# A transformer block pair on one Trainium2 core: other ring buffers and another order for the FFN's and the modulation's weights, and block products for a 1024x1024 projection

## The reference, cut to what matters

```python
# first block: gated FFN with a causal three-tap convolution, F = 2816
up, gate = h @ w_up            # 1024 x 5632, 22 feature tiles of 128, twice
g = silu(conv3(gate_half)) * other_half
x = x + g @ w_down
# second block: modulation by silu(c) and silu(c_ctx)
mod_lat = silu(c) @ w_mod + b_mod        # 1024 x 6144, all six parts
mod_ctx = silu(c_ctx) @ w_mod + b_mod    # only the first third is used
# second block: convolution branch
y = silu(layer_norm(depthwise_conv31(glu(u))))   # 512 x 1024
y_c = y @ w_pw                                   # 1024 x 1024
out = (sigmoid(g_a) * y_a + sigmoid(g_c) * y_c) @ w_out
```

## Time and profile before

| | us |
|---|---|
| median of 3 runs | 2852.98 (2847.22 to 2857.23) |
| the profiled execution | 2857.41, of which the span from first to last instruction 2856.1 |
| up projection, from unit 1 to the first down product | 432.90 to 697.43 |
| last gates and layer norm to the start of the w_pw product | 1094.6 to 1128.11 |
| w_pw product, norms of the latents | 1128.11 to 1187.22 |
| attention, first PEER tiles | 1187 to 1508 |
| PEER | 1508 to 2856 |

### The profile page before, as it was taken

The page is one execution under the profiler, slowest core; times in us unless marked ns, Lnnn a source line. Parts: engine busy times, 40 slices in busy tenths (PEclk is TensorE's granted clock), DMA queues, the critical chain, the costliest instruction groups (busy, mean ns, idle before and its releaser), DMA issues.

```text
span 2856.1 us, 24271 instructions
## 1 busy us (share of the span) xinstructions
PE 2551.8 (89%) x8286; PEld 1395.8 (49%) x8286; DVE 1713.8 (60%) x3704; ACT 648.4 (23%) x1588; POOL 679.1 (24%) x574
## 2 busy tenths in 40 slices
PE   8999989999999999999998989799877777777776
PEld 5655458887444443466665544365322323232222
DVE  1132449988116993366545676766675767667555
ACT  2223220001011002266412221322121221222112
POOL 0000032332000000000002344444443444444342
PEclk9999999999999999999999999999999999999999
DMA  4101023344212211000249999999999999999997
GB/s 160 59 30 47 13 111 148 148 177 177 103 54 97 89 72 62 15 1 30 88 154 370 420 420 419 405 420 420 420 420 420 420 420 420 420 420 420 420 420 295
DMA packets 87305, 687.01 MB, mean 241 GB/s; under 512 B 9976, under 2 KB 10616, under 8 KB 12816
## 3 DMA queue, kind: packets, MB, share of 16 engines
q0 software_dynamic: 73728, 536.90, 45.5%
q1 hardware_dynamic: 12016, 143.99, 13.1%
q10 hardware_dynamic: 1440, 4.57, 0.4%
HBM read 683.32 MB, written 2.10 MB: 240 GB/s over the span
## 4 chain that ended last, share of the span: by engine, by line
PE 46%; DMA 27%; DVE 5%; ACT 2%; issue 1%; POOL 0%; ACTq 0%; DVEq 0%; POOLq 0%
PE psum L400 21%; DMA weights<-in_experts,expert 16%; PE psum L1113 11%; DMA slot<-in_experts,expert 10%; PE psum L914 3%; PE psum L1007 2%; PE psum L865 2%; PE psum L985 2%; PE psum L936 2%; PE psum L975 2%; PE psum L922 1%; DVE weights L2265 1%; DVE slot L2265 1%; DMA xn<-in_experts,expert 1%; ACT spare_row L1582 1%
## 5 line engine op out<-in xcount | busy, mean ns | idle before, releaser
L1113 PE MATMUL psum<-weights,spare_row 128*128 128x512 f32 x832 | 386.5, 607 | 106.5 <-ACT spare_row L1582 104.3
L1113 PE MATMUL psum<-slot,spare_row 128*128 128x512 f32 x844 | 401.6, 612 | 49.8 <-ACT spare_row L1582 49.7
L2339 POOL DMA_INDIRECT slot<-in_experts,expert x211 | 223.8, 1061 | 577.1 <-DVE expert L2212 304.6
L2265 DVE CUSTOM_DVE_ANT_0 slot<-slot,hT 128x1024 f32<-128x1024 f32 x211 | 257.4, 1223 | 164.3 <-DMA slot<-in_experts,expert 163.0
L2265 DVE CUSTOM_DVE_ANT_0 weights<-weights,hT 128x1024 f32<-128x1024 f32 x208 | 253.5, 1223 | 147.6 <-DMA weights<-in_experts,expert 146.6
L1113 PEld LDWEIGHTS psum<-weights,spare_row 128*128 128x128 f32 x832 | 152.6, 191 | 327.8 <-ACT spare_row L1582 171.5
L2339 POOL DMA_INDIRECT weights<-in_experts,expert x208 | 223.0, 1072 | 298.3 <-PE psum L1113 290.0
L1113 PEld LDWEIGHTS psum<-slot,spare_row 128*128 128x128 f32 x844 | 162.8, 196 | 261.2 <-issue 184.1
L1577 ACT ACTIVATE coef<-hidden 128x2 f32<-128x2 f32 (+1 forms) x257 | 52.2, 203 | 977.6 <-DVE hidden L2265 977.6
L1113 PE MATMUL psum<-xn,spare_row 128*128 128x512 f32 x372 | 188.2, 630 | 86.4 <-ACT spare_row L1582 86.4
L400 PE MATMUL psum<-xnT,weights 128*128 128x264 f32 (+1 forms) x1040 | 246.4, 392 | 6.7 <-DVE gT L1828 2.8
(11 more groups left out here) (361 smaller groups left out, 3279.1 us busy)
## 6 DMA issues: line engine op xcount, KB each, us to landing
weights<-in_w_mod SPq DMA_DIRECT2D x12, 2048.0 KB, 8.3
weights<-in_w_up SPq DMA_DIRECT2D x11, 2048.0 KB, 7.7
weights<-in_w_in SPq DMA_DIRECT2D x8, 2048.0 KB, 8.3
weights<-in_w_pq SPq DMA_DIRECT2D x8, 2048.0 KB, 11.5
weights<-in_w_out SPq DMA_DIRECT2D x6, 2048.0 KB, 9.2
weights<-in_w_in_t SPq DMA_DIRECT2D x4, 2048.0 KB, 7.7
weights<-in_w_down SPq DMA_DIRECT2D x4, 2048.0 KB, 8.4
weights<-in_w_o_mla SPq DMA_DIRECT2D x4, 2048.0 KB, 9.9
```

The costliest lines, as they stand in the source:

```text
L1113: last = pe.matmul(acc.pair[:, half, :], k.diags[pick % 8], k.slots[slot][:, D + half * 512:D + (half + 1) * 512], start=h0 == 0 and j == ...
L2265: ins = dve.tensor_tensor_reduce(slot[:, 0:D], slot[:, 0:D], k.h2[:, i, :], 1.0, 0.0, ALU.mult, ALU.add, hid[:, j:j + 1])
L2339: pool.indirect_dma_start(k.slots[slot], None, k.A["experts"], bass.IndirectOffsetOnAxis(ap=k.expert[b % 2][:, j:j + 1], axis=0))\
```

## The change

Four edits.

1. Ring: the up units take buffers 2 and 0 in turn, and the modulation's units buffer 1 alone. SyncE's order becomes up 0, up 1, mod 0, up 2, mod 1, ...: each up unit one place earlier. The modulation's units are taken in `MOD_ORDER`, so that two-row units (16 instructions) and one-row units (8) alternate.
2. Product order in an up unit: 1, 5, 6, 7, 2, 3, 4 in place of 1, 6, 5, 7, 2, 3, 4, product 5 waiting for s1 alone; GpSimd's sums for unit 1 wait until VectorE has made t1 to t4.
3. `ln_sq`, the PE product that VectorE's sum of squares must precede, goes behind the first tile of `gates(3)`.
4. The w_pw product in block form: per pair of output tiles `q` seven products of 4 matmuls with 256 columns; GpSimd makes the sums of w_pw's blocks (of the first unit once `ln_sq_sum` is complete, of the second once `gates(3)` is done, since they lie over `hT`), VectorE those of the tokens' blocks after the last Silu. ScalarE copies product 1 out, VectorE adds the others. The three latent norms all move into `q` = 2. The attention's `values2` on ScalarE waits for `pw_gated` in place of the last w_pw tile.

```diff
+MOD_ORDER = (0, 4, 1, 5, 2, 6, 3, 7, 8, 9, 10, 11)
+    def mod_rows_of(self, turn):
+        return MOD_ORDER[turn], sum(2 if m < 4 else 1 for m in MOD_ORDER[:turn])
 def ffn_up():            # tensor
+        k.ring.order, k.ring.at = [2, 0, 1] + (NF // 2 - 3) // 2 * [2, 1, 0, 1] + [2, 1, 1], 0
+        k.up_units, k.mod_units = [k.ring.turn()], []
         for u_ in range(NF // 2):
-            unit, w = weights(KC, 512)
-            k.ring.turn()
+            if u_ + 1 < NF // 2:
+                k.up_units.append(k.ring.turn())
+            k.mod_units.append(k.ring.turn())
+        k.ring.order, k.ring.at = [0, 1, 2], 0
...
+                pe.wait_ge(s.up_sum, 4 * u_ + 1)
+                if u_ == 0:
+                    pe.wait_ge(s.up_xsum, 1)
+                product((u_, h, 5), left(sums[0], h), t1)
                 pe.wait_ge(s.up_sum, 4 * u_ + 2)
...
                 product((u_, h, 6), left(sums[1], h), t2)
-                product((u_, h, 5), left(sums[0], h), t1)
 def latents_and_norm():  # tensor
-        u = take("ln_sq")
-        pe.wait_ge(s.ln_sq_sum, KC - 1)
-        pe.matmul(u.pair[:, 0, :], k.ones[:], k.ln_sum, start=True, stop=True).then_inc(u.fill())
-        gates(3)
+        def squares():
+            ...
+        gates(3, squares)    # called behind the first of its four tiles
 def conv_out():          # tensor
+        def product(q, x, left, right, reads=1):
+            u = take(("pw", q, x), reads)
+            chain(u.pair[:, 0, 0:SEQ // 2], [(left[:, c, q % 2, :], right[:, c, :]) for c in range(KC // 2)]).then_inc(u.fill())
+        for q in range(4):
+            product(q, 1, blocks[0], low_left)     # q == 0: then product 2
+            pe.wait_ge(s.pw_sum, q // 2 * 4 + 2)
+            product(q, 5, s1, t1)
+            product(q, 6, s2, t2)
+            if q == 2: feature_norm("n_cq", SEQ, 0, 2)
+            pe.wait_ge(s.pw_sum, q // 2 * 4 + 4)
+            product(q, 7, blocks[2], t3, reads=2)
+            if q: product(q, 2, blocks[1], high_left)
+            if q == 2: feature_norm("n_ckv", SEQ, 2, 1)
+            product(q, 3, s4, high_right)
+            u = product(q, 4, blocks[3], t4)
+            if q == 2: feature_norm("n_ckv_c", CTX, 3, 1)
+            if q == 1: swap()
 def ffn_up():            # vector
-            some(mods, 3 if 0 < u_ < 5 else 2)
+            some(mods, 3 if u_ and MOD_ORDER[u_ - 1] < 4 else 2)
...
-            some(mods, 4 if u_ < 4 else 2)      # twice
+            some(mods, 4 if MOD_ORDER[u_] < 4 else 2)
 def conv_out():          # vector
+        dve.wait_ge(s.ln_silu, KC)
+        dve.tensor_tensor(t1[:], low_right, low_left, ALU.subtract).then_inc(s.pw_xsum)
+        ...                                  # t2, t3 (in place), t4: 128 x 1024 each
+        def blocks(q):
+            plus(k.pw_both[:], k.pw_first[q % 2][:], u[6])
+            plus(one[1], k.pw_both[:], u[5])
+            yield
+            plus(two[1], one[1], u[7]); plus(k.pw_both[:], k.pw_both[:], u[7])
+            plus(one[0], k.pw_first[q % 2][:], u[2])
+            yield
+            plus(one[1], one[1], u[3]);  gated(2 * q, u[2], u[3])
+            plus(two[0], k.pw_both[:], u[4]);  gated(2 * q + 1, u[4])
 def gpsimd_program(k):
         elif u_ == 1:
             pool.wait_ge(*of["xnT2", NT - 1].full[1])
+            pool.wait_ge(s.up_xsum, 4)
         else:
-            pool.wait_ge(*k.ring_done[unit - 4])
+            pool.wait_ge(*k.ring_done[k.up_units[u_ - 2]])
+    for u_ in range(2):
+        pool.wait_ge(s.ln_sq_sum, KC - 1)
+        pool.wait_ge(*k.arrived(k.pw_units[u_]))
+        if u_:
+            pool.wait_ge(*of["gate", 2 * KC - 1].full[-1])
+        ...                                  # s1, s2, low0 - low1, s4, as in ffn_up
 def sync_program(k):
+    weights("w_up", 0)
     for unit in range(NF // 2):
-        weights("w_up", unit)
-        weights("w_mod", unit)
+        if unit + 1 < NF // 2:
+            weights("w_up", unit + 1)
+        weights("w_mod", MOD_ORDER[unit])
```

More of the change, by code:

```diff
@@ L812, in conv_in, with gates @@
             gates(u_)
-    def gates(u_):
+    def gates(u_, behind_first=k.nothing):
         unit, w = weights(KC, 512)
@@ L854, in swap @@
             pe.matmul(u.pair[R, 0, :], k.swap2[R, R], k.kr[R, 0:SEQ], start=True, stop=True).then_inc(u.fill())
-        between = {3: swap, 4: lambda: feature_norm("n_cq", SEQ, 0, 2), 5: lambda: feature_norm("n_ckv", SEQ, 2, 1),
-                   6: lambda: feature_norm("n_ckv_c", CTX, 3, 1)}
-        for n in range(KC):
-            if n % 4 == 0:
-                unit, w = weights(KC, 512)
-            u = take(("pw", n))
-            for c in range(KC):
-                if n == 0:
-                    pe.wait_ge(s.ln_silu, c + 1)
-                last = pe.matmul(u.pair[:, 0, :], w[:, c, n % 4 * P:(n % 4 + 1) * P], k.padded[:, c, 0:SEQ], start=c == 0, stop=c == KC - 1)
-            last.then_inc(u.fill())
+        low_left, low_right, high_left, high_right = k.pw_windows()
@@ L867, in conv_out @@
             k.ring_done[unit] = u.full[-1]
-            if n in between:
-                between[n]()
+            if q == 1:
+                swap()
     def attention():
@@ L1389, in conv_out, with first @@
     def conv_out():
+        def first(q):
+            if q > 1:
+                act.wait_ge(*of["pw", q - 2, 2].free)
+            copy_out(("pw", q, 1), k.pw_first[q % 2][:], of["pw", q, 1].pair[:, 0, 0:SEQ // 2])
+        for q in range(3):
+            first(q)
         act.wait_ge(s.kr, 1)
@@ L1442, in attention @@
         queries(0)
[L1443 removed]
+        act.wait_ge(s.pw_gated, KC)
         values2()
@@ L1773, in mixer, with mod_sums @@
                 add_out(1, half, i)
-    def mod_sums(m):
-        unit = k.mod_unit(m)
+    def mod_sums(turn):
+        m, first = k.mod_rows_of(turn)
+        unit = k.mod_units[turn]
         w = k.weight(unit)[:].rearrange("p (k n) -> p k n", k=KC)
@@ L2001, in conv_out @@
     def conv_out():
-        for n in range(KC):
-            u = of["pw", n]
-            dve.wait_ge(*u.full[-1])
-            dve.tensor_tensor(k.merged[:, n, :], u.pair[:, 0, :], k.sig_c[:, n, :], ALU.mult).then_inc(u.out)
-            if n != 3:
+        low_left, low_right, high_left, high_right = k.pw_windows()
+        t1, t2, t4 = k.pw_xsums
+        dve.wait_ge(s.ln_silu, KC)
+        dve.tensor_tensor(t1[:], low_right, low_left, ALU.subtract).then_inc(s.pw_xsum)
+        dve.wait_ge(s.pw_xsum, 1)
@@ new lines, in conv_out, with plus, gated @@
+        dve.tensor_tensor(t2[:], high_right, t1[:], ALU.subtract).then_inc(s.pw_xsum)
+        dve.tensor_tensor(low_right, high_right, low_right, ALU.subtract).then_inc(s.pw_xsum)
+        dve.wait_ge(s.pw_xsum, 2)
+        dve.tensor_tensor(t4[:], high_left, t2[:], ALU.subtract).then_inc(s.pw_xsum)
+        def plus(dst, left, u):
+            dve.wait_ge(*u.full[-1])
+            dve.tensor_tensor(dst, left, u.pair[:, 0, 0:SEQ // 2], ALU.add).then_inc(u.out)
+        def gated(n, *made):
+            for u in made:
+                dve.wait_ge(*u.free)
+            dve.tensor_tensor(k.merged[:, n, :], k.merged[:, n, :], k.sig_c[:, n, :], ALU.mult).then_inc(s.pw_gated)
@@ new lines, in blocks @@
+        def blocks(q):
+            u = {x: of["pw", q, x] for x in range(1, 8)}
+            one, two = ([k.merged[:, n, a:a + SEQ // 2] for a in (0, SEQ // 2)] for n in (2 * q, 2 * q + 1))
+            dve.wait_ge(*u[1].free)
+            plus(k.pw_both[:], k.pw_first[q % 2][:], u[6])
+            dve.wait_ge(*u[6].free)
+            plus(one[1], k.pw_both[:], u[5])
+            yield
+            dve.wait_ge(*u[5].free)
+            plus(two[1], one[1], u[7])
+            plus(k.pw_both[:], k.pw_both[:], u[7])
+            plus(one[0], k.pw_first[q % 2][:], u[2])
+            yield
+            plus(one[1], one[1], u[3])
+            gated(2 * q, u[2], u[3])
+            dve.wait_ge(*u[7].free)
+            plus(two[0], k.pw_both[:], u[4])
+            gated(2 * q + 1, u[4])
+            yield
@@ new lines, in conv_out @@
+        for q in range(4):
+            steps = blocks(q)
+            next(steps)
+            if q == 2:
+                feature_norm("n_cq", [k.cq[:, 0, :], k.cq[:, 1, :]], SEQ, [col(k, "q_g", 0), col(k, "q_g", 1)], k.feature_root[0])
+            next(steps)
+            if q == 2:
+                feature_norm("n_ckv", [k.ckv[:, 0:SEQ]], SEQ, [col(k, "kv_g")], k.feature_root[1])
+            next(steps)
+            if q == 2:
+                feature_norm("n_ckv_c", [k.ckv[:, SEQ:NKV]], CTX, [col(k, "kv_g")], k.feature_root[2])
+            if q != 1:
```

78 lines of the change are left out of this document (62 added, 16 removed).

## The result

The changed kernel takes 2834.99 us (median of 4 runs, 2831.57 to 2836.62) against 2854.51 (4 runs of the kernel before, 2847.22 to 2857.23): ratio 0.9935, 95% interval 0.9923 to 0.9948, or 19.5 us less. The forecast was 2838, 15 us less. The profiled execution took 2831.57, with a span of 2830.3 against 2856.1, 25.8 us less.

A forecast was written before the change was run, and what follows sets the result against it. PE sets the time before 2000 us, with VectorE nearly as full in the up projection; DMA gathers bound it after. Terms -3.5 - 5.1 - 6.6 = -15.2 us from 2857.41 give 2842.2, or 2838 against the median 2852.98; range 2826 to 2850.

The forecast's parts named there:

- The layer norm's sum: Before w_pw: a gate tile ahead of the squares' product fills PE's 3.40 us gap; -5.1 us, bounds -5.2 and -3.
- The forecast's worst case: Layer norm: GpSimd's sums block the reciprocal and first scaling, token sums end by 1124; cover said to hold by 4 us.
- The w_pw product: Block form: 224 matmuls of 0.217 us take 48.6 us in place of 55.1; -6.6 us, bounds -6.9 and -3.
- The rival that w_pw isn't bound by PE: w_pw is bound by what surrounds it, so its 6.6 us don't come: 2845 us, chance 0.12.
- Unit 0: Up projection: token sums run alone, PE resumes 4.3 us earlier and regains full rate; -6.1 us, bounds -3.5 and -6.3.
- The rival in which the gap stays: Up projection, unit 0: the gap stays because t1 isn't faster alone: 2844 us, chance 0.05.
- Units 1 to 10: Up projection: waits on GpSimd go, waits for VectorE come; stalls 11.4 us in place of 8.8, +2.6; bounds -8.8 and +19.
- the walk: Unit-by-unit timing of VectorE beside GpSimd in the up projection: 3.5 us stall in unit 1, 1.9 in 4, 2.7 in 5.
- A rule against the change: Shared SBUF ports: by the skill's lock rule each GpSimd instruction could wait out a whole VectorE one; rows show about half.
- the slow case: Up projection: GpSimd waits 0.75 us per instruction, VectorE needs 31 us a unit against PE's 25.7: 2863 us, chance 0.04.
- The rival of no stalls: Up projection: VectorE keeps up and no unit stalls; 26.6 us gained in all, 2826 us, chance 0.20.
- The rival of 3.5 us in each unit: Up projection: VectorE sets the pace, 3.5 us stall in each of units 1 to 8, +19; 2854 us, chance 0.11.

The follow-up runs named there:

- e2: The kernel before with only the norm and w_pw edits (3 and 4), up stage as before: 2839.32 us, ratio 0.9958.
- e5: The changed kernel with the first FFN convolution tap moved from VectorE to ScalarE and the second half's shared addition ahead of the convolution: 2828.77 us, ratio 0.9928.
- e12: The changed kernel with the squares' product ahead of the gates again: 2841.95 us, ratio 0.9964.
- e1: The kernel before with only the up projection's edits (1 and 2), norm and w_pw as before: 2850.09 us, ratio 0.9993.
- e6: The changed kernel run again without further change, on the same chip as its variants: 2831.52 us, ratio 0.9937.
- e11: The changed kernel with the old product order 1, 6, 5 in the up units: 2832.46 us, ratio 0.9932.

## Why the prediction was right, point by point

**The layer norm's sum**: right in mechanism and size (-5.1; 36.36 or 36.37 us in every trace with the edit in place of 41.2 to 41.5). The price named, squares later and Silu later, is there, and the cover holds by more than forecast: the token sums end 8 us before PE asks for t1. The forecast's worst case, by its own times (sums done at 1124, t1 wanted at 1126.5), left 2.5 and not the 4 it names.

**The w_pw product**: right (-6.6; 52.52 or 52.53 us in every trace with the edit). PE never waits in it. The forecast feared q = 2 most and put VectorE's end of it at 1170.5 with w_pw's start at 1123, 47.5 us behind it; measured is 1159.6 with the start at 1112.31, 47.3. The rival that w_pw isn't bound by PE fell with this.

**Unit 0**: right in mechanism, too small in size, -7.7 against -6.1 and outside its bounds by 1.4. The forecast's own two terms (411.81 - 407.5, and 5.63 - 3.5) add up to 6.4, so -6.1 is 0.3 too small by its own terms, and the bound of -6.3 is too small as well. t1 alone is 1.23 us, inside the 1.1 to 1.5 estimated, and the instructions behind the gap regained their rate as said. The 1.6 us missed lie ahead of both: in the kernel before PE's first 16 instructions of the stage took 5.38 us at 398.66, in the one after 3.71. They took 3.71 in e2 too, with the up stage as before, and 5.39 in e5 and e12, which have the changed one, so this is no effect of the change. The same sum, made from e2, is 11.48 to 7.32 for the restart plus 6.28 to 3.72 for the instructions behind, -6.7. That is still 0.4 us past the bound. The rival in which the gap stays fell in all eleven traces with both halves of the edit.

**Units 1 to 10**: the forecast total was near and the walk behind it was wrong. Waits for GpSimd went, as said; those for VectorE came, 6.9 us and 1.5 more for the slower instructions behind the longest. Against the 255.7 without stalls the stage is 9.5 us longer, where 11.4 was forecast. But the walk put the large ones in units 1, 4 and 5, and they came in 1 and 3, with 0.35 and 1.13 us in 7 and 8. In unit 1 all three of its first sums had started before GpSimd did, at +8.35 us (433.32) and not +7.8, so `right5` was in time and only `right7` late, 1.54 us in place of 3.5. In unit 3 VectorE came in at +7.8 (485.75) where the walk had +5.5, behind the start of GpSimd's first instruction and not before it, and the `right5` forecast for +13.0 came at +19.2 (497.20). The step that failed is the state carried from unit to unit. The other traces of this up stage say that this is not chance alone: in all four VectorE is done with the gates at +6.8 to +10.2 of unit 3, and PE stalls there for 3.0 to 4.6 us where the walk had none; in units 4 and 5 it is done at +4.1 to +6.0 where the walk had +6.8 and +6.6, and PE stalls for 0.24 us at most where the walk had 1.9 and 2.7. That the total came out near (9.5 for 11.4) is therefore luck in part: the 4.6 us forecast for units 4 and 5 didn't come, and 3.9 us with 1.5 more behind them came in unit 3, where none were forecast. Beyond that a walk can't be sure of single units: in unit 3 only 0.6 us decide between VectorE's sum and GpSimd's (485.75 and 485.15), the point on which, as the forecast says itself, all hangs, and single waits for modulation weights are longer (1.96 us at 454.86). The range for the total (from all stalls gone to 19 more) was wide against what four traces span, 6.5 us.

**A rule against the change.** The traces show VectorE held (50 us of held time in the up stage). GpSimd's instructions start 2.3 to 2.4 us apart alone (1087.28, 1094.31 and the two between) and up to 3.0 beside VectorE, mostly 2.6 to 2.8, so 0.3 to 0.6 us more and not the 0.75 of a whole VectorE instruction each time; the slow case that rested on it, 2863, fell. The Trainium skill (SBUF — State Buffer, "Who interferes with whom") has the pair of ports locked for the whole instruction by whichever engine came first, and the other fully blocked. This is no evidence against that rule: a held sum ends 0.3 to 0.55 us behind GpSimd's instruction, and that is about what GpSimd's next one waits. What failed is the 0.75 that the slow case took for each wait.

**The rival of no stalls** (2826) isn't this change, but it is a measured kernel: 2827.07 and 2826.87 us, once with VectorE relieved and once with GpSimd. **The rival of 3.5 us in each unit** (+19 in the stage) comes nearest with the plain order of modulation units, +10.4 in units 1 to 10 against the kernel before.

**The sum.** 15.2 us less forecast, 18.8 in the changed stretches of the one trace, 19.5 between medians. The 3.6 us between forecast and trace are 1.6 in unit 0, nearly all of it outside the terms of the forecast, and 2.0 in units 1 to 10. One thing stays open: the parts, timed alone, give 0.9 and 11.7 us, together 12.6, and the whole gives 19.5 and 21.7 in its two comparisons. The intervals meet at their edges (up to 5.4 for the first part and 16.5 for the second), and e1's own trace shows its up stage 4.8 us shorter and its span 13.4 shorter than before's, so it may be the spread of the unchanged stages; it wasn't settled. The medians thus show the gain of the second block, and that the whole gains 15 to 22 us; the gain of the up stage's edits rests on the traces.

## What to carry to other kernels

Where two engines hold each other, a walk over their phases is worth little for single stalls: here some came back in each trace, others only in some, and the walk missed both kinds, though its total was near. Forecast the total from what is busy and what is held, and give one of the engines slack, since in this kernel either a lighter VectorE or a lighter GpSimd removed every stall. Moving two additions, as here, only moved the stalls. A wait on the critical engine is best filled with work that stands right behind it (one gate tile ahead of the squares' product): beside the w_pw product that was the surest part of the change, 36.4 us in place of 41.2 to 41.5 in each trace. Moving loads earlier, in a stage where VectorE is nearly full, won nothing that these runs can tell over the small edit beside it. And an edit that helps at one place (product 5 second, in unit 0) should also be tried at that place alone: in the units that repeat it may cost what it wins.

## What the runs showed of the hardware that was not expected

- VectorE's hold beside GpSimd isn't only for two operands in SBUF: a TENSOR_SCALAR of 128x512 with one took 2.50 us at 485.75 beside GpSimd's 485.15 to 487.96, and 0.48 where GpSimd is idle (454.86). The RECIPROCAL of 128x512, also with one, took 3.35 us at 1092.63 beside two GpSimd instructions, and 3.35 with GpSimd idle (1145.47): it isn't held. Additions with one operand in PSUM keep their 0.42.
- A stall can cost more than its length, and not by a fixed sum: behind 1.54 us of it eight instructions took 2.00 instead of 1.90, hardly more than behind a fold with no stall at all (1.98); behind 3.91 they took 3.44, behind 3.02 (e6) 3.64, and behind 3.18 (e1) again no more than 1.98; behind 2.27 (e11) sixteen took 5.40 instead of 3.64; and behind 3.40 (e12) the clock stood at 0.50 for some 6 us.
- Unchanged code takes one of a few values. From the first down product to the mean it was 385.8, 387.5 or 389.2 us, 1.7 apart, in fourteen traces; what picks the value wasn't found (the granted clock from 755 to 860 us was 0.98 in one trace with 389.2 and 1.00 in another).
